# First layer's sample attention: value pages begun by the weights' queue in turn with the key pages, none by GpSimd

## The reference, cut to what matters

```python
def diff_attn_core(q, ks, vs, masks, lam, lam_init, subln_g):
    logits = jnp.concatenate([jnp.einsum('bqhmd,bkhmd->bhmqk', q, k) for k in ks], axis=-1) * (HD_B ** -0.5)
    logits = jnp.where(jnp.concatenate(masks, axis=-1), logits, -jnp.inf)
    p = jax.nn.softmax(logits, axis=-1)
    a = p[:, :, 0] - lam * p[:, :, 1]
    ...                                   # o = a @ v over past and new values, then an RMS norm per head

kv_past = cache_b_kv[i][page_table].reshape(Bs, past_len, 2, H_B, 2 * HD_B)   # gather by page
k_past, v_past = kv_past[:, :, 0], kv_past[:, :, 1]                          # keys, values
```

## Time and profile before

| | |
|---|---|
| median of 3 runs | 1908.63 us |
| profiled execution, own time | 1901.55 us |
| its span | 1900.0 us |
| TensorE matmul busy | 1806.1 us (95%) |
| TensorE weight load busy | 1665.9 us (88%) |
| VectorE, ScalarE, GpSimd busy | 938.4, 593.2, 233.4 us |
| hardware DMA queue (SP) | 216.18 MB, 34.6% of 16 engines' span |
| software DMA queue (GpSimd) | 120.97 MB, 17.6% |
| mean granted TensorE clock | 0.981 |

### The profile page before, as it was taken

The page is one execution under the profiler, slowest core; times in us unless marked ns, Lnnn a source line. Parts: engine busy times, 40 slices in busy tenths (PEclk is TensorE's granted clock), DMA queues, the critical chain, the costliest instruction groups (busy, mean ns, idle before and its releaser), DMA issues.

```text
span 1900.0 us, 38089 instructions
## 1 busy us (share of the span) xinstructions
PE 1806.1 (95%) x15237; PEld 1665.9 (88%) x15237; DVE 938.4 (49%) x1415; ACT 593.2 (31%) x1102; POOL 233.4 (12%) x350
## 2 busy tenths in 40 slices
PE   5997898899999999999979999999999999999998
PEld 4995665689999999999868888878889999999998
DVE  5335676445444343534434454576774534344444
ACT  3114555433222121231333353363223222222222
POOL 3512333211000000020000000003002000000002
PEclk9998999899999999999989999999999999999999
DMA  6228999514776766625147747743132676522221
GB/s 194 75 84 281 328 332 318 191 45 155 265 243 232 253 242 242 243 89 200 58 137 239 240 156 239 238 151 112 46 108 77 211 251 241 213 90 88 89 79 59
DMA packets 176173, 338.83 MB, mean 178 GB/s; under 512 B 10698, under 2 KB 117892, under 8 KB 174445
## 3 DMA queue, kind: packets, MB, share of 16 engines
q1 hardware_dynamic: 163573, 216.18, 34.6%
q0 software_dynamic: 12480, 120.97, 17.6%
HBM read 324.33 MB, written 100.19 MB: 223 GB/s over the span
## 4 chain that ended last, share of the span: by engine, by line
PE 85%; DVE 6%; DMA 4%; ACT 2%; issue 2%; SPq 1%; POOLq 0%; POOL 0%; DVEq 0%; ACTq 0%
PE pp L636 53%; PE pp L882 16%; PE pp L696 2%; PE pp L992 2%; DMA vring<-in_cache_b_kv 2%; PE pp L1039 2%; PE pp L1005 1%; PE pp L733 1%; PE pp L709 1%; DVE rnorm L1169 1%; PE pp L1020 1%; DMA out_new_d_prompt<-pt_l 1%; ACT e_p L1913 1%; PE pp L682 1%; PE pp L1064 1%
## 5 line engine op out<-in xcount | busy, mean ns | idle before, releaser
L1741 ACT ACTIVATE whi<-raw 128x1024 fp32r<-128x1024 f32 x208 | 220.6, 1061 | 868.3 <-PE pp L636 723.7
L636 PE MATMUL pp<-a_hi,whi 128*128 128x288 f32 x1280 | 277.3, 298 | 10.3 <-DVE wlo L1141 5.6
L636 PE MATMUL pp<-a_lo,whi 128*128 128x288 f32 x1280 | 276.4, 298 | 0.0
L1141 DVE TENSOR_TENSOR wlo<-raw,whi 128x1024 fp32r<-128x1024 f32 x208 | 258.4, 1242 | 36.0 <-ACT whi L1741 36.0
L636 PE MATMUL pp<-a_hi,wlo 128*128 128x288 f32 x1280 | 276.2, 298 | 0.0
L636 PE MATMUL pp<-b_hi,whi 128*128 128x288 f32 x1280 | 274.4, 296 | 0.3 <-DVE zbuf L1414 0.3
L636 PE MATMUL pp<-b_lo,whi 128*128 128x288 f32 x1280 | 274.1, 296 | 0.0
L636 PE MATMUL pp<-b_hi,wlo 128*128 128x288 f32 x1280 | 274.1, 296 | 0.0
L636 PEld LDWEIGHTS pp<-a_hi,whi 128*128 128x128 f32 x1280 | 208.3, 190 | 11.4 <-DVE wlo L1141 6.3
L636 PEld LDWEIGHTS pp<-a_hi,wlo 128*128 128x128 f32 x1280 | 208.6, 191 | 0.0
L636 PEld LDWEIGHTS pp<-a_lo,whi 128*128 128x128 f32 x1280 | 208.4, 191 | 0.0
(11 more groups left out here) (242 smaller groups left out, 2118.6 us busy)
## 6 DMA issues: line engine op xcount, KB each, us to landing
out_new_d_sample<-in_cache_d_kv POOLq DMA_DIRECT2D x32, 2040.0 KB, 8.5
kring<-in_cache_b_kv SPq DMA_DIRECT2D x128, 256.0 KB, 4.6
vring<-in_cache_b_kv POOLq DMA_DIRECT2D x128, 256.0 KB, 4.9
raw<-in_w_up SPq DMA_DIRECT2D x32, 1024.0 KB, 5.4
raw<-in_w_down SPq DMA_DIRECT2D x32, 1024.0 KB, 5.2
kring<-in_cache_d_kv SPq DMA_DIRECT2D x104, 256.0 KB, 3.1
vring<-in_cache_d_kv SPq DMA_DIRECT2D x104, 256.0 KB, 4.4
raw<-in_w_in_cd SPq DMA_DIRECT2D x24, 1024.0 KB, 5.3
```

What stands on the lines that cost most here:

```text
L636: last = pe.matmul(acc_h[s][:, h, :], w[s][:, k, :], m[:, k, NH * h:NH * h + NH], start=(at_ == 0 and n == 0), stop=(at_ == KT_N - 1 and n ...
L1141: dve.tensor_tensor(wlo_v[j], raw_v[q // 2][:, :, j, :], whi_v[j].bitcast(F32), ALU.subtract).then_inc(wlo_ready, 1)
L1741: act.activation(whi_v[j], raw_v[q // 2][:, :, j, :], ACT.Copy).then_inc(whi_ready, 1)
```

## The change

SP issues the value half blocks too. In `cache_blocks`, step i of sequence b now issues the first half of the key block two steps ahead, then both halves of the value block of this step, then the second half of the key block. The values of block (0, 0) are issued by SP before the weights, behind the keys of that block, and left out in the sequence. GpSimd issues no pages of this stage any more; it only stages the queries. Buffers, semaphores, waits for slots, sizes and the other engines' programs stay the same.

```diff
                 def sequence(b):
                     for i in range(4):
                         after = (b, i + 2) if i < 2 else None if isinstance(b, int) and b == NB - 1 else (b + 1, i - 2)
-                        for half in range(2 if after else 0):
-                            load_block(sp, 0, *after, half)
+                        if after:
+                            load_block(sp, 0, *after, 0)
+                        for half in range(0 if isinstance(b, int) and b == i == 0 else 2):
+                            load_block(sp, 1, b, i, half)
+                        if after:
+                            load_block(sp, 0, *after, 1)
...
             load_block(sp, 0, 0, 0, 0)
             load_block(sp, 0, 0, 0, 1)
+            load_block(sp, 1, 0, 0, 0)
+            load_block(sp, 1, 0, 0, 1)
             matrix(w_ab, T_AB, 16, first=1)
...
-                def values(b, i):
-                    load_block(pool, 1, b, i, 0)
-                    load_block(pool, 1, b, i, 1)
-
-                stage(0)
-                pool.wait_ge(tile_done, T_AB + 16)
                 for b in range(NB):
-                    if b:
-                        values(b, 0)
-                    values(b, 1)
-                    if b < NB - 1:
-                        stage(b + 1)
-                    values(b, 2)
-                    values(b, 3)
+                    stage(b)
                 pool.wait_ge(S0["q"], 2 * NB)
...
             sum_squares(0)
-            pool.wait_ge(s_page, 16)
-            load_block(pool, 1, 0, 0, 0)
-            load_block(pool, 1, 0, 0, 1)
             link(pool.memset(pool_a[:, :, 0:16], 0.0))
```

## The result

| | before | after |
|---|---|---|
| median | 1907.14 us (4 runs) | 1997.05 us (4 runs, 1984.76 to 2001.46) |
| ratio, 95% interval | | 1.0464 [1.0424, 1.0503] |
| profiled execution, own time | 1901.55 us | 1995.76 us |
| span | 1900.0 us | 1994.2 us |
| GpSimd busy | 233.4 us | 164.8 us |

A forecast was written before the change was run, and what follows sets the result against it. Transfers bound sample attention before, SP's issuing after: 122 half blocks, 291.6 us, put the last value page 91.1 us later, other terms 0. The runs' median 1908.63 + 91 gives 2000 us, range 1976 to 2022.

The forecast's parts named there:

- The bound of the stage: First layer's sample attention: SP's issuing sets the pace, 39.2 us per sequence in place of 26.2; chance 0.86.
- Start: Value pages (0, 0) on SP before the weights: 4.3 us of issuing fit into 6.8 us of slack, cost 0.
- The sum over SP's half blocks: Sample attention: 122 half blocks take SP 291.6 us, so the last value page is issued 91.1 us later.
- Unrolled first part: SP's first sequence in sample attention: 14 half blocks at 2.165 us, 30.3 us.
- loop: SP's six looped sequences: 96 half blocks at 2.42 us plus six turns at 0.5 us, 235.3 us.
- the last DMA: SP's last value-page DMA in sample attention: issued at 449.8 us, where it was 358.7.
- The lower end of a value half block: Cheapest cost assumed for a value half block in SP's loop: 2.35 us, which would give +84 us.
- The tail: End of sample attention, last value issue to last product: stays 5.3 us, at most 2 us either way.
- Behind the stage: After sample attention: everything moves as a block; the output projection's third weight unit lands in 5.4 us, hidden, cost 0.
- Bandwidth as the bound: Rival in sample attention: SP's issuing hides under the transfers, a sequence stays at 26 us, 1909 us; chance 0.05.
- the faster case: Rival in sample attention: TensorE's stalls on value pages go, at most 13.4 us, 1895 us; chance 0.03.
- The clock: Sample attention: TensorE's clock falls in part at no cost; as rival, low throughout, 48 us more, 2048; chance 0.06 above 2022.

The follow-up runs named there:

- the knee: Kernel after with GpSimd keeping part of the value pages: SP issuing half of them 1933.14 us (ratio 1.0156), a quarter 1905.96 us (0.9997).
- the extra read: One more unused page-table read per half block on SP: in the kernel after 2063.36 us (1.0851), in the kernel before 1907.49 us (0.9998).
- the kernel without lookups: Kernel after with SP taking pages in the order of their numbers, without reading the page table: 1893.55 us, ratio 0.994.

## Why the prediction was right

**The bound of the stage.** It was SP's instruction stream, as predicted. The chain and the missing waits for slots say so, and the knee, the extra read and the kernel without lookups show it.

**Start.** Value pages (0, 0) cost nothing: the weights behind them started at 35.12 us in place of 34.63, with the four value DMAs issued at 29.82 to 32.87 ahead of them (timeline of SP):

```profile
25.41 3.08 SPq L420 DMA_DIRECT2D kring<-in_cache_b_kv  x4
29.82 3.05 SPq L420 DMA_DIRECT2D vring<-in_cache_b_kv  x4
35.12 0.38 SPq L456 DMA_DIRECT2D raw<-in_w_in_ab  x1
```

SP's third half block began at 159.08 us, 0.8 earlier than in the earlier trace rows.

**The sum over SP's half blocks.** Unrolled first part 31.2 us (159.08 to 190.32) for 30.3 predicted; loop 233.8 us (190.32 to the first half block behind it, 424.15) for 235.3; the last DMA at 449.05 for 449.8. The total is right to 1 us, but within the loop by luck, for two parts were wrong and cancelled. The lower end of a value half block was put at 2.35 us; single DMA starts of SP in the loop show less:

```profile
212.07 0.33 SPq L420 DMA_DIRECT2D vring<-in_cache_b_kv  x1
...
214.25 0.33 SPq L420 DMA_DIRECT2D vring<-in_cache_b_kv  x1
...
216.66 0.33 SPq L420 DMA_DIRECT2D kring<-in_cache_b_kv  x1
...
219.98 1.12 SPq L420 DMA_DIRECT2D kring<-in_cache_b_kv  x1
```

From 212.07 to 214.25 it is 2.18 us, as cheap as unrolled; to the next half block it is 2.41. In the loop's second sequence, in which no DMA instruction was held up (229.9 to 268.1 us), the half blocks took 2.18 to 2.58 us, and 2.81 with the turn: 38.2 us, 1 us less than the 39.2 predicted. What the prediction did not have is a DMA instruction that takes 1.1 to 1.6 us in place of 0.33. Four of the six sequences had one and took 39.3 to 39.5. The view of L420, 150 to 455 us, gives the extremes (ns, min/median/max):

```profile
L420 SPq DMA_DIRECT2D kring<-in_cache_b_kv x124: 332/333/1559, 154.7 to 440.3; - x124
...
L420 SPq DMA_DIRECT2D vring<-in_cache_b_kv x124: 332/333/1572, 165.6 to 449.1; - x124
```

So 2.42 with 0.5 per turn gave the right total with half blocks some 0.06 us too dear and no slow instruction. The "2.35 to 2.5 us" that the prediction wanted to see holds for the mean (2.39 over all of them), not for the single half block.

**The tail** was mis-sized by 2.4 us, more than the "at most 2" allowed. From the last value issue to the last product it was 7.7 us (449.05 to 456.13 + 0.65), not 5.3. The rows at the end, from timelines of SP and TensorE:

```profile
449.05 0.33 SPq L420 DMA_DIRECT2D vring<-in_cache_b_kv  x1
449.43 0.43 SPq L456 DMA_DIRECT2D raw<-in_w_out_ab  x1
...
454.67 0.64 PE L739 MATMUL pp<-vring,pt_l 128*32 128x128 f32 x16 [1.13 <-DMA vring<-in_cache_b_kv]
...
456.13 0.65 PE L739 MATMUL pp<-qkv_s,pt_l 64*32 64x128 f32 x8 [0.55 <-DVE samp L1287]
...
483.91 0.53 PE L642 MATMUL pp<-b_hi,whi 128*128 128x288 f32 x2
```

The last value page landed 5.6 us after its issue where 2.9 was the median, later than every other page that SP issued in the stage, with the 1 MB weight unit issued 0.4 us behind it. The unit itself took 8.0 us, for 5.4 in the earlier trace rows. With SP's sequences written out and with twice the work on TensorE, where the order is the same, the last page took 5.2 and 5.5 us. Before, SP issued that unit 11 us ahead of the last value pages. The prediction asked whether the unit would be late, not whether it would delay the page ahead of it. That the unit did so is argued from the order; it is not shown, for no run took the unit away.

**Behind the stage.** The output projection began at 483.91, 94.2 us later than in the earlier trace rows: 92.7 from the stage's end and 1.5 more in between, where the clock was at its low level (0.50 granted) from 455.8 to 483.1 us; before, it was so from 364.9 to 385.4 only. From there to the end both spans have 1510.3 us. So the profiled execution moved by 94.2 us for 91.1 predicted: 0.8 less by SP's last issue, 2.4 more in the tail, 1.5 more behind it. The median moved by 89.9. The 4 us between the two are spread: the execution profiled before was 5.6 us faster than the median of the runs, the one after 1.3 us.

**The rivals.** Bandwidth as the bound and the faster case needed a half block of 1.64 us on SP, and the cheapest was 2.16. The rule of the Trainium skill ("DMA: Bandwidth & Descriptors", Issuing engines are not separate DMA queues), that issuing time is usually small beside the DMA, would have given no change; with the lookups that belong to each issue it was the largest term here. The same section of the Trainium skill says that DMAs run on the same 16 DMA engines, whichever engine started them. The run without lookups agrees: one queue moved 331 GB/s, two had moved 327. The clock did fall in parts of the stage, as expected, at no cost until the stage's end.

## What to carry to other kernels

Before moving DMAs to another engine, add up that engine's sequencer time per period, with lookups, register steps and loop arithmetic and not the DMA instructions alone, and compare it with the period of what bounds the stage. A page of busy shares does not show this time; the starts of unstalled issues do. Here moving was free up to the knee, and beyond it every added instruction was paid in full. Shorter landings with longer waits for them say that the issue is late.

## What the runs showed of the hardware beyond that

- An indexed load of one 256 KB page cost SP about 1.1 us, of which the DMA instruction was 0.33; reading four table entries at once took 0.30 us in place of 4 x 0.27, but the register step and the check behind each number stayed (0.15 and 0.02 us, and the gaps).
- Four of the 248 DMA instructions that SP issued in the stage took 1.1 to 1.6 us in place of 0.33, with the DMA engines busy only 0.7 of the time. What held it up is open.
- TensorE's granted clock fell to 1.2 GHz (0.5) and rose again 18 times between 150 and 450 us, a stage in which it was busy 28 to 30 of 39.2 us with gaps for the pages; with part of its work done twice it was granted 0.91 to 0.92 on average, in place of 0.82 to 0.87.
